# A 2-layer hybrid diffusion step on one core: the attention stage's products with the values moved between the two scores of a group

## The chip, the cores and the metric

The kernel runs on one core of one Trainium2 chip. The metric is device microseconds (us) of one launch; lower is better. The engines are named as in the trace: PE is TensorE (PEld its weight loads), DVE is VectorE, ACT is ScalarE, POOL is GpSimd, and SP is SyncE, which here only starts DMAs. Each engine works through its own list of instructions in the order in which the program wrote it, and waits between engines are semaphores that count up.

## The reference, cut to what matters

The step has two layers: a long gated convolution with its feed-forward block, and then a neighbourhood attention with its feed-forward block. Only the attention of the second layer is touched. 16 heads of 64 values each attend over 1024 latent tokens on a 16 x 64 grid; a block of queries sees a window of local keys and all 256 cached context keys in one softmax. The 256 prompt tokens of the same layer attend among themselves.

```python
s_loc = einsum('bhrjqd,bhrjkd->bhrjqk', qb, kg) + bias
s_loc = where(valid, s_loc, -inf)
s_ctx = einsum('bhrjqd,bhkd->bhrjqk', qb, k_ctx)
p = softmax(concatenate([s_loc, s_ctx], axis=-1))
o = p[..., :nk] @ vg + p[..., nk:] @ v_ctx
```

## The kernel before

All matrices go through TensorE as a high and a low part (`_hi`, `_lo`), so that a product of two of them is three matmuls. The attention is one stage of the program (lines 1973 to 2343). It takes the heads in 8 pairs `i`. A pair has U = 20 units `u` of 128 queries, 10 for each head of the pair, and G = 10 groups `g` of two units. In each head, groups 0 to 3 are local (640 scores a query: 256 of the context and 384 of the window), and group 4 is the prompt (256 scores a query). Five groups, thus one head, are called a half here; there are 16 halves in the stage.

A unit passes through these steps, each a function of its own:

- `scores` (PE, L2126): six matmuls, or two for the prompt, into `ps_s[u % 2]`.
- `minima` (DVE, L2292): bias and mask are added and the row minimum of the negated scores taken; the result lies in `probs`.
- `exps` (ACT, L2198): the exponential with its row sum, in place.
- `recip` (DVE, L2299) and `norm` (POOL, L2261): division by the sum. POOL also makes the bias of later units (`bias_mask`, L2252).
- `turn_local` (three transposes a unit into `ps_l`) and `turn_ctx` (four a group into `ps_c`), both PE, L2130.
- `high_local`, `high_ctx` (ACT, L2204, L2211) and `low_local`, `low_ctx` (DVE, L2303, L2308): the transposed numbers split into `pt_hi` and `pt_lo`.
- `mix` (PE, L2171), once a group: the products with the values, 18 matmuls for a local group and 6 for the prompt, into `ps_o`, of which there is one.
- `out_high` (ACT, L2217) and `out_low` (DVE, L2315): `ps_o` is read out into `a_hi` and `a_lo`. `mix(i, g)` waits on the semaphore `ol_ok` until `out_low` of group g - 1 is through, since it writes `ps_o` anew. It also waits on `ll_ok` and `lc_ok` for its own `pt_lo`.

`run` (L2052) calls one function `step(i, g, last)` on each engine, in the same sequence; what stands in an engine's `step` is the order of its queue. Step g of PE makes the scores of group g + 1, turns group g and mixes group g - 1. ACT's step g is `high_local(2g)`, `exps(2g + 2)`, `high_local(2g + 1)`, `high_ctx(g)`, `exps(2g + 3)`, `out_high(g - 1)`. DVE's step g is the following, where `out_low` is two groups back:

```python
if scored(g, last):
    minima(i, 2 * g + 2)
if g >= 2:
    out_low(i, g - 2)
if turned and local(2 * g):
    low_local(i, 2 * g)
if scored(g, last):
    minima(i, 2 * g + 3)
    recip(i, 2 * g + 2)
```

After these come `low_local(2g + 1)`, `low_ctx(g)` and `recip(2g + 3)`; at the last group of a pair `out_low(9)` stands at the end of the step.

Of the kernel before, what the change touches and what calls it, by code (L numbers as in the profile page):

```python
# [53 lines left out]
def hyena_natten_step(nc, t):  # L54
    ctx = ExitStack()
    with ctx:
# [1916 lines left out]
        with stage() as st:  # L1973
# [30 lines left out]
            def unit(u):  # L2004

                hh, n = u % U // 10, u % 10
                return (hh, n // 2, n % 2) if n < 8 else (hh, None, n - 8)

            def local(u):
                return unit(u)[1] is not None  # L2010

            def locals_before(u):

                return sum(local(v) for v in range(u))

            def unit_at(i, c):
                return i * U + c

            def local_at(i, c):
                return i * 16 + c  # L2020

            def group_at(i, c):
                return i * G + c
# [28 lines left out]
            def run(eng, prologue, step):  # L2052

                prologue()
                step(0, 0, False)
                for i in range(7):
                    for g in range(1, G + 1):
                        step(i, g, False)
                for g in range(1, G + 1):
                    step(7, g, True)  # L2060

            def scored(g, last):

                return not (last and g >= G - 1)
# [42 lines left out]
            def _(pe):  # L2107
# [21 lines left out]
                def turn(dst, u, b):  # L2129
                    return pe.transpose(dst, pb[:, u % U % 4, 128 * b:128 * b + 128], ident[:, :])  # L2130

                def turn_local(i, u):
                    pe.wait_ge(pn_ok, unit_at(i, u + 1))
                    if u >= 2:
                        pe.wait_ge(ll_ok, local_at(i, locals_before(u - 1)))
                    for b in range(3):
                        last = turn(ps_l[u % 2][:, 128 * b:128 * b + 128], u, 2 + b)
                    last.then_inc(tl_mm, 1)

                def turn_ctx(i, g):  # L2140
                    if g:
                        pe.wait_ge(lc_ok, group_at(i, g))
                    for half in range(2):
                        pe.wait_ge(pn_ok, unit_at(i, 2 * g + half + 1))
                        for b in range(2):
                            last = turn(ps_c[:, 256 * b + 128 * half:256 * b + 128 * half + 128], 2 * g + half, b)
                        last.then_inc(tc_mm, 1)

                def mix(i, g):
                    hh, j, _ = unit(2 * g)  # L2150
                    if g == 0:
                        pe.wait_ge(v_in[4 + i % 2], 16 * (i // 2) + 16)
                    if hh == 0:
                        if j is None:
                            pe.wait_ge(v_in[6 + i % 2], 16 * (i // 2) + 16)
                        else:
                            pe.wait_ge(v_in[j], i * 64 + 64)
                    if j is not None:
                        pe.wait_ge(ll_ok, local_at(i, locals_before(2 * g + 2)))
                    pe.wait_ge(lc_ok, group_at(i, g + 1))  # L2160
                    pe.wait_ge(ol_ok, group_at(i, OL0 + g))
                    s, c = 6 * (g % 2), 14 + 4 * (g % 2)
                    v0 = (16 if j is not None else 18) + 4 * (i % 2)
                    uses = [(v0, c, 0, 256)]
                    if j is not None:
                        uses += [(4 * j, s, 0, 128), (4 * j + 3, s + 7, 128, 128), (4 * j + 1, s + 2, 0, 256),
                                 (4 * j + 2, s + 4, 0, 256)]
                    uses += [(v0 + 1, c + 2, 0, 256)]
                    for n, (b, x0, q0, nq) in enumerate(uses):
                        for term, (hl, x) in enumerate(((0, pth), (0, ptl), (1, pth))):  # L2170
                            last = pe.matmul(ps_o[:, q0:q0 + nq], vt[:, b, hl, :],  # L2171
                                             x[:, x0:x0 + nq // 128, :].rearrange("p a b -> p (a b)"),
                                             start=n == 0 and term == 0, stop=n == len(uses) - 1 and term == 2)
                    last.then_inc(pv_mm, 1)
# [6 lines left out]
                def step(i, g, last):  # L2181
                    for half in range(2):
                        if scored(g, last):
                            scores(i, 2 * g + 2 + half)
                        if local(2 * g) and not (last and g == G):
                            turn_local(i, 2 * g + half)
                    if not (last and g == G):
                        turn_ctx(i, g)
                    if g:
                        mix(i, g - 1)  # L2190
                run(pe, prologue, step)

            @block.scalar
# [85 lines left out]
            @block.vector  # L2279
            def _(dve):  # L2280
                def minima(i, u):
                    w = width(u)
                    dve.wait_ge(s_mm, unit_at(i, u + 1))
                    if local(u):
                        dve.wait_ge(bm_ok, local_at(i, locals_before(u) + 1))
                    else:
                        dve.wait_ge(bm_ok, local_at(i, locals_before(u)))
                    before = u - 4
                    if before >= 0:
                        dve.wait_ge(tc_mm, unit_at(i, before + 1))  # L2290
                    dve.sem_inc(turn_v, 1)
                    dve.tensor_tensor_reduce(out=pb[:, u % U % 4, 0:w], in0=ps_s[u % 2][:, 0:w], in1=bm[:, u % 2, 0:w],  # L2292
                                             scale=1.0, scalar=3.0e38, op0=ALU.add, op1=ALU.min,
                                             accum_out=stat[:, u % 4, 0:1]).then_inc(sm_ok, 1)

                def recip(i, u):
                    q = stat[:, u % 4, :]
                    dve.wait_ge(p_exp, unit_at(i, u + 1))
                    dve.reciprocal(q[:, 2:3], q[:, 1:2]).then_inc(rr_ok, 1)  # L2299

                def low_local(i, u):
                    dve.wait_ge(hl_ok, local_at(i, locals_before(u) + 1))
                    dve.tensor_tensor(p_loc(ptl, u), ps_l[u % 2][:, 0:384].rearrange("p (b n) -> p b n", n=128),  # L2303
                                      p_loc(pth, u).bitcast(F32), ALU.subtract).then_inc(ll_ok, 1)

                def low_ctx(i, g):
                    dve.wait_ge(hc_ok, group_at(i, g + 1))
                    dve.tensor_tensor(p_ctx(ptl, g), ps_c[:, :].rearrange("p (b n) -> p b n", n=128),  # L2308
                                      p_ctx(pth, g).bitcast(F32), ALU.subtract).then_inc(lc_ok, 1)

                def out_low(i, g):
                    dve.wait_ge(oh_ok, group_at(i, g + 1))
                    dst, src = views(a_l, i, g)
                    hi = views(a_h, i, g)[0]
                    dve.tensor_tensor(dst, src, hi.bitcast(F32), ALU.subtract).then_inc(ol_ok, 1)  # L2315

                def prologue():
                    dve.sem_inc(ol_ok, OL0)
                    minima(0, 0)
                    minima(0, 1)  # L2320
                    recip(0, 0)
                    recip(0, 1)

                def step(i, g, last):
                    turned = not (last and g == G)
                    if scored(g, last):
                        minima(i, 2 * g + 2)
                    if g >= 2:
                        out_low(i, g - 2)
                    if turned and local(2 * g):  # L2330
                        low_local(i, 2 * g)
                    if scored(g, last):
# [3 lines that stand above are left out]
                        low_local(i, 2 * g + 1)  # L2336
                    if turned:
                        low_ctx(i, g)
                    if scored(g, last):
                        recip(i, 2 * g + 3)  # L2340
                    if g == G:
                        out_low(i, G - 1)
                run(dve, prologue, step)

        stage_rest(1, e0)
# [143 lines left out]
```

## Time and profile before

| | us |
|---|---|
| median of 3 runs | 3808.89 (3808.26 to 3813.37) |
| the profiled execution, device time | 3808.96 |
| its span in the trace | 3807.1 |
| attention stage in it, first scores to last product | 2322.1 to 2695 |
| PE busy over the whole span | 3598.1 (95%) |

A stage of the program ends with a barrier, so what the attention stage gains or loses is added to the whole one for one. In a row of the timeline the first number is the start and the second the duration, both in us; a matmul's end is a modelled one, and matmuls overlap, so that the distance between two starts tells more than one duration. What stands in brackets is how long the engine had been idle, and which instruction released it.

### The profile page before, as it was taken

How to read it: one execution, taken by the hardware profiler on the slowest of the kernel's cores; microseconds unless marked ns; L12 is line 12 of the kernel's file. 1: busy time of each engine (PE TensorE's matmuls, PEld its weight loads, DVE VectorE, ACT ScalarE, POOL GpSimd, SP SyncE). 2: the span in 40 equal slices, each digit the busy share in tenths (PEclk: the TensorE clock that was granted, in tenths of full speed). 3: DMA queues.
4: the chain of work that ended last, by engine and by line, in shares of the span. 5: the costliest groups of instructions: out<-in, count | busy, mean ns of one | idle time of the engine just before them, and what ended most of it. 6: DMA issues, size and time to landing. Idle time of an engine off the chain costs nothing. (4 is left out here: it accounts for less than half of the span.)

```text
span 3807.1 us, 47310 instructions
## 1 busy us (share of the span) xinstructions
PE 3598.1 (95%) x19244; PEld 3065.7 (81%) x19244; DVE 1515.6 (40%) x2472; ACT 1033.6 (27%) x1554; POOL 1230.0 (32%) x815
## 2 busy tenths in 40 slices
PE   8999998898899999999989998999899999999997
PEld 6788887677788888888868877888778888888885
DVE  2765553454524444434451014777341122111116
ACT  1441111132421111111152224777433111111113
POOL 1531113623532222222361213666343222222223
PEclk9999999999999999999999999999999999999998
DMA  3253323754122122221234355777201111111111
GB/s 118 87 168 117 105 90 134 247 187 145 49 72 67 61 78 72 76 68 62 77 120 161 144 174 158 179 178 171 84 28 39 35 39 39 39 38 35 39 39 61
DMA packets 178710, 369.58 MB, mean 97 GB/s; under 512 B 17063, under 2 KB 102567, under 8 KB 176840
## 3 DMA queue, kind: packets, MB, share of 16 engines
q1 hardware_dynamic: 173064, 356.21, 29.7%
q10 hardware_dynamic: 5440, 10.49, 0.9%
q8 instruction: 146, 2.39, 0.3%
q14 instruction: 60, 0.49, 0.0%
HBM read 286.93 MB, written 79.69 MB: 96 GB/s over the span
## 5 line engine op out<-in xcount | busy, mean ns | idle before, releaser
L148 POOL TENSOR_TENSOR w_lo<-w_raw,w_hi 128x1024 fp32r<-128x1024 f32 x210 | 506.0, 2410 | 1509.1 <-ACT w_hi L142 1509.1
L156 PE MATMUL ps_r<-a_hi,w_hi 128*128 128x512 f32 (+1 forms) x2496 | 640.4, 358 | 17.1 <-POOL a_lo L1716 11.4
L156 PE MATMUL ps_r<-a_hi,w_lo 128*128 128x512 f32 (+1 forms) x2496 | 635.8, 356 | 0.0
L156 PE MATMUL ps_r<-a_lo,w_hi 128*128 128x512 f32 (+1 forms) x2496 | 635.6, 356 | 0.0
L142 ACT ACTIVATE w_hi<-w_raw 128x1024 fp32r<-128x1024 f32 (+1 forms) x217 | 225.3, 1038 | 1018.3 <-PE ps_r L156 563.4
L156 PEld LDWEIGHTS ps_r<-a_hi,w_hi 128*128 128x128 f32 x2496 | 415.2, 188 | 100.3 <-POOL a_lo L1716 19.2
L156 PEld LDWEIGHTS ps_r<-a_lo,w_hi 128*128 128x128 f32 x2496 | 415.1, 188 | 74.0 <-issue 1.5
L156 PEld LDWEIGHTS ps_r<-a_hi,w_lo 128*128 128x128 f32 x2496 | 415.1, 188 | 73.6
L1909 DVE TENSOR_TENSOR hid_l<-hid_l,ps_r 128x1280 f32<-128x1280 f32 x44 | 65.5, 1488 | 840.7 <-PE ps_r L156 840.7
L1929 DVE SCALAR_TENSOR_TENSOR x_t_l<-ps_r,mod,x_t_l 128x1024 f32<-128x1024 f32 (+1 forms) x288 | 241.4, 880 | 264.6 <-PE ps_r L156 264.6
L1756 POOL TENSOR_TENSOR hid_lo_l<-hid_l,hid_hi_l 128x1280 fp32r<-128x1280 f32 x42 | 134.4, 3201 | 488.1 <-ACT hid_hi_l L1657 488.1
L156 PE MATMUL ps_in<-x_split_f,w_hi 128*128 128x512 f32 (+1 forms) x1152 | 259.7, 361 | 2.6 <-DVE gout_f L571 2.6
L1846 DVE CUSTOM_DVE_ANT_0 ps_x<-ada_w_l,silu_c_l 128x1024 f32<-128x1024 f32 x116 | 198.4, 1710 | 110.0 <-DMA ada_w_l<-in_ada_t 107.5
L156 PEld LDWEIGHTS ps_in<-x_split_f,w_hi 128*128 128x128 f32 x1152 | 192.2, 191 | 36.5 <-DVE gout_f L571 2.8
L156 PE MATMUL ps_r<-hid_hi_l,w_lo 128*128 128x512 f32 (+1 forms) x864 | 214.2, 355 | 0.0
L156 PE MATMUL ps_r<-hid_hi_l,w_hi 128*128 128x512 f32 (+1 forms) x864 | 214.2, 355 | 0.0
L156 PE MATMUL ps_r<-hid_lo_l,w_hi 128*128 128x512 f32 (+1 forms) x864 | 214.2, 355 | 0.0
L1657 ACT ACTIVATE hid_hi_l<-hid_l 128x1280 fp32r<-128x1280 f32 x44 | 56.1, 1274 | 541.8 <-DVE hid_l L1909 541.8
L1651 ACT ACTIVATE hid_l<-ps_r 128x1280 f32<-128x1280 f32 x44 | 54.6, 1240 | 455.2 <-PE ps_r L156 455.2
L2171 PE MATMUL ps_o<-pt_hi,v_hl 128*128 128x256 f32 (+1 forms) x832 | 166.6, 289 | 7.6 <-DVE a_lo L2315 7.6
L1461 PE MATMUL ps_r<-a_hi,w_hi 128*128 128x512 f32 (+1 forms) x384 | 144.2, 376 | 23.6 <-PEq L78 14.1
L156 PEld LDWEIGHTS ps_r<-hid_lo_l,w_hi 128*128 128x128 f32 x864 | 142.1, 188 | 25.5
(227 smaller groups left out, 6038.2 us busy)
## 6 DMA issues: line engine op xcount, KB each, us to landing
w_raw<-in_w_all SPq DMA_DIRECT2D x213, 512.0 KB, 3.6
ada_w_l<-in_ada_t SPq DMA_DIRECT2D x59, 512.0 KB, 3.5
v_hl<-v_d SPq DMA_DIRECT2D x128, 128.0 KB, 2.9
t_tail_f<-in_ada_t SPq DMA_DIRECT2D x24, 512.0 KB, 4.2
spec<-gout_f SPq DMA_DIRECT2D x80, 128.0 KB, 2.1
g_spec_c<-spec ACTq DMA_DIRECT2D x20, 512.0 KB, 5.7
y_d<-y_spec_c SPq DMA_DIRECT2D x40, 256.0 KB, 3.5
v_d<-z_v_l SPq DMA_DIRECT2D x10, 1024.0 KB, 4.6
```

What stands on the lines that cost most here:

```text
L142: act.activation(wh[:, s, 0:width], raw[:, s, 0:width], ACT.Copy).then_inc(w_hi, 1)
L148: pool.tensor_tensor(wl[:, s, 0:width], raw[:, s, 0:width], wh[:, s, 0:width].bitcast(F32), ALU.subtract).then_inc(w_split, 1)
L156: last = pe.matmul(out[:, c0:c1], w[:, c % 2, blk * 128:blk * 128 + 128], x[:, c0:c1], start=start and b == 0 and term == 0, stop=stop and ...
L1461: last = pe.matmul(bank(n, c1 - c0), w[:, (e0 + m) % 2, k * 128:k * 128 + 128], x[:, k, c0:c1], start=k == 0 and term == 0, stop=k == KT - ...
L1651: act.activation(sg[:, :], pg[0][:, 0:TOK], ACT.Silu).then_inc(silu, 1)
L1657: act.activation(hh[:, i % 2, k, :], sg[:, :], ACT.Copy).then_inc(hh_ok, 1)
L1756: pool.tensor_tensor(hl[:, i % 2, k, :], sg[:, :], hh[:, i % 2, k, :].bitcast(F32), ALU.subtract).then_inc(hl_ok, 1)
L1846: dve.tensor_tensor_reduce(out=px[:, :], in0=w[:, :], in1=vec[:, q, :], scale=1.0, scalar=0.0, op0=ALU.mult, op1=ALU.add, accum_out=acc_a[ ...
L1909: dve.tensor_tensor(sg[:, :], sg[:, :], pg[1][:, 0:TOK], ALU.mult).then_inc(gated, 1)
L1929: ins = dve.scalar_tensor_tensor(xt[:, m, p0:p1], pg[m % 2][:, p0:p1], gate[:, p:p + 1], xt[:, m, p0:p1], ALU.mult, ALU.add)
L2171: last = pe.matmul(ps_o[:, q0:q0 + nq], vt[:, b, hl, :], x[:, x0:x0 + nq // 128, :].rearrange("p a b -> p (a b)"), start=n == 0 and term = ...
```

## The change

On PE the products with the values of group g - 1 move from the end of step g to a place behind the transposes of the group's first unit, between the two scores. On DVE `out_low(g - 2)` moves ahead of the first `minima` of the step. ACT, POOL and SP keep their lists as they are.

```diff
@@ -2184,10 +2184,10 @@
                             scores(i, 2 * g + 2 + half)
                         if local(2 * g) and not (last and g == G):
                             turn_local(i, 2 * g + half)
+                        if g and half == 0:
+                            mix(i, g - 1)
                     if not (last and g == G):
                         turn_ctx(i, g)
-                    if g:
-                        mix(i, g - 1)
                 run(pe, prologue, step)
@@ -2323,10 +2323,10 @@
                 def step(i, g, last):
                     turned = not (last and g == G)
+                    if g >= 2:
+                        out_low(i, g - 2)
                     if scored(g, last):
                         minima(i, 2 * g + 2)
-                    if g >= 2:
-                        out_low(i, g - 2)
                     if turned and local(2 * g):
                         low_local(i, 2 * g)
```

PE's list, at a step that makes the prompt's scores (two matmuls each). Before, from the first transposes to the start of the mix:

```order
L2126 MATMUL ps_s<-k_hl_193_16730,q_hl_192_16729 128x256 x2
L2130 MATMUL ps_l<-ident,probs_16724 128x128 x3
L2126 MATMUL ps_s<-k_hl_193_16730,q_hl_192_16729 128x256 x2
L2130 MATMUL ps_l<-ident,probs_16724 128x128 x3
L2130 MATMUL ps_c<-ident,probs_16724 128x128 x4
L2171 MATMUL ps_o<-pt_hi_16725,v_hl_16723 128x256
```

The same step in the changed program, with the first and the last matmul of the mix:

```order
L2126 MATMUL ps_s<-k_hl_193_16730,q_hl_192_16729 128x256 x2
L2130 MATMUL ps_l<-ident,probs_16724 128x128 x3
L2171 MATMUL ps_o<-pt_hi_16725,v_hl_16723 128x256
...
L2171 MATMUL ps_o<-pt_hi_16725,v_hl_16723 128x256
L2126 MATMUL ps_s<-k_hl_193_16730,q_hl_192_16729 128x256 x2
L2130 MATMUL ps_l<-ident,probs_16724 128x128 x3
L2130 MATMUL ps_c<-ident,probs_16724 128x128 x4
```

The mix now stands ahead of one score, three transposes and the four context transposes that it stood behind.

DVE's list at the seam of two local steps, before (L2292 is `minima` and the reading of its result, L2315 `out_low`, L2303 `low_local`, L2308 `low_ctx`):

```order
L2308 TENSOR_TENSOR pt_lo_16726<-ps_c,pt_hi_16725 128x512
L2299 RECIPROCAL stat_16728<-stat_16728 128x1
L2292 ISA probs_16724,stat_16728<-ps_s,bias_m_16727 128x640
L2292 ISA stat_16728 128x1
L2315 TENSOR_TENSOR a_lo<-ps_o,a_hi 64x16x16
L2303 TENSOR_TENSOR pt_lo_16726<-ps_l,pt_hi_16725 128x3x128
```

and in the changed program:

```order
L2308 TENSOR_TENSOR pt_lo_16726<-ps_c,pt_hi_16725 128x512
L2299 RECIPROCAL stat_16728<-stat_16728 128x1
L2315 TENSOR_TENSOR a_lo<-ps_o,a_hi 64x16x16
L2292 ISA probs_16724,stat_16728<-ps_s,bias_m_16727 128x640
L2292 ISA stat_16728 128x1
L2303 TENSOR_TENSOR pt_lo_16726<-ps_l,pt_hi_16725 128x3x128
```

`out_low` changed places with one `minima`; what lies before and behind the two is the same. ACT's list, which is the same in both programs, ends a local step like this (L2204 is `high_local`, L2211 `high_ctx`, L2198 `exps`, L2217 `out_high`):

```order
L2204 ACTIVATE pt_hi_16725<-ps_l 128x3x128
L2211 ACTIVATE pt_hi_16725<-ps_c 128x512
L2198 ACTIVATE probs_16724,stat_16728<-probs_16724,stat_16728 128x640
L2217 ACTIVATE a_hi<-ps_o 64x16x16
```

## Rows read from the trace of the kernel before

**Rows 1.** Windows: two halves; busy PE, PEld, DVE, ACT, POOL, clock, DMA, GB/s.

```profile
2466.54:2511.42 44.88, 41.47 (x348) 39.99 (x348) 34.12 (x96) 31.88 (x76) 28.40 (x36) 1.00 0.73 175
```

**Rows 2.** Waits in the attention stage: us in total, times, longest us.

```profile
PE ps_l L2130 <- POOL probs L2261: 21.2, 47, 0.7
...
PE ps_o L2171 <- DVE a_lo L2315: 7.6, 16, 1.0
```

**Rows 3.** Timeline of all engines, last steps of a half and first of the next.

```profile
2505.34 0.40 PE L2126 MATMUL ps_s<-k_hl,q_hl 128*128 128x256 f32 x2
...
2511.42 0.43 DVE L2315 TENSOR_TENSOR a_lo<-ps_o,a_hi 64x256 fp32r<-64x256 f32 x1
...
2512.00 0.35 PE L2171 MATMUL ps_o<-pt_hi,v_hl 128*128 128x256 f32 x1 [0.50 <-DVE a_lo L2315]
...
2512.37 0.60 ACT L2211 ACTIVATE pt_hi<-ps_c 128x512 fp32r<-128x512 f32 x1
...
2513.00 0.69 DVE L2308 TENSOR_TENSOR pt_lo<-ps_c,pt_hi 128x512 fp32r<-128x512 f32 x1 [0.21 <-ACT pt_hi L2211]
```

**Rows 4.** Timeline of all engines, the local step that follows.

```profile
2514.17 0.82 PE L2126 MATMUL ps_s<-k_hl_l,q_hl_l 128*128 128x256 f32 x6
...
2515.09 0.90 PE L2126 MATMUL ps_s<-k_hl_l,q_hl_l 128*128 128x256 f32 x6
2515.20 0.82 DVE L2292 CUSTOM_DVE_ANT_0 probs<-ps_s,bias_m 128x640 f32<-128x640 f32 x1 [1.23 <-PE ps_s L2126]
...
2515.37 0.49 ACT L2204 ACTIVATE pt_hi<-ps_l 128x384 fp32r<-128x384 f32 x1 [0.62 <-PE ps_l L2130]
...
2516.07 0.83 ACT L2198 ACTIVATE probs<-probs,stat 128x640 f32<-128x640 f32 x1 [0.21 <-DVE stat L2292]
...
2516.17 0.60 PE L2130 MATMUL ps_c<-ident,probs 128*128 128x128 f32 x4
...
2516.64 0.35 PE L2171 MATMUL ps_o<-pt_hi,v_hl 128*128 128x256 f32 x1
...
2517.00 0.81 DVE L2292 CUSTOM_DVE_ANT_0 probs<-ps_s,bias_m 128x640 f32<-128x640 f32 x1
...
2517.43 0.82 PE L2126 MATMUL ps_s<-k_hl_l,q_hl_l 128*128 128x256 f32 x6
...
2518.11 0.80 POOL L2261 TENSOR_SCALAR probs<-probs,stat 128x640 f32<-128x640 f32 x1 [1.08 <-DVE stat L2299]
...
2518.80 0.38 ACT L2217 ACTIVATE a_hi<-ps_o 64x256 fp32r<-64x256 f32 x1
...
2518.96 0.55 PE L2130 MATMUL ps_l<-ident,probs 128*128 128x128 f32 x3 [0.71 <-POOL probs L2261]
...
2519.22 0.43 DVE L2315 TENSOR_TENSOR a_lo<-ps_o,a_hi 64x256 fp32r<-64x256 f32 x1 [0.19 <-ACT a_hi L2217]
```

**Rows 5.** Timeline of ACT alone, the end of a local step.

```profile
2494.31 0.47 ACT L2204 ACTIVATE pt_hi<-ps_l 128x384 fp32r<-128x384 f32 x1
2494.68 0.59 ACT L2211 ACTIVATE pt_hi<-ps_c 128x512 fp32r<-128x512 f32 x1
2495.16 0.82 ACT L2198 ACTIVATE probs<-probs,stat 128x640 f32<-128x640 f32 x1
...
2495.97 0.37 ACT L2217 ACTIVATE a_hi<-ps_o 64x256 fp32r<-64x256 f32 x1
```

**Rows 6.** Timeline, the stage's first half: its first `low_ctx`.

```profile
2331.41 0.69 DVE L2308 TENSOR_TENSOR pt_lo<-ps_c,pt_hi 128x512 fp32r<-128x512 f32 x1 [0.40 <-ACT pt_hi L2211]
```

**Rows 7.** Timeline, the first `minima` of the stage's second half.

```profile
2350.16 0.82 DVE L2292 CUSTOM_DVE_ANT_0 probs<-ps_s,bias_m 128x640 f32<-128x640 f32 x1 [5.64 <-POOL bias_m L2252]
```

**Rows 8.** Timeline of PE, the last mix of the stage.

```profile
2694.47 0.35 PE L2171 MATMUL ps_o<-pt_hi,v_hl 128*128 128x256 f32 x1 [1.02 <-DVE a_lo L2315]
```

**Rows 9.** Windows, columns as in Rows 1: a window with idle time, one at low clock.

```profile
1010.00:1015.00 5.00, 3.07 (x15) 2.19 (x13) 5.00 (x9) 3.43 (x5) 5.00 (x4) 1.00 0.00 0
...
2350.00:2355.00 5.00, 3.85 (x17) 3.48 (x18) 2.93 (x8) 2.33 (x5) 4.90 (x7) 0.50 1.00 239
```

## The prediction, made before the changed kernel was run

> **What bounds the kernel now.** I first asked for the busy time of a steady piece of the attention stage, since the change touches no other. Two halves (two heads) last 44.88 us, and PE is busy for 41.47 us of it, 92%, at the full granted clock, 1.00; DVE is busy 34.12 us, ACT 31.88 us and POOL 28.40 us [rows 1]. A half therefore takes 22.44 us and PE bounds it. Then I read the waits of the stage: what PE loses is 21.2 us in 47 transposes that came before POOL had normalised the unit, and 7.6 us in 16 mixes that waited for `out_low` [rows 2]. Together that is 28.8 us, and no reordering of PE can win more than about that here. Last I read the timeline of single steps, because the change shifts a mix by a fraction of a step and the answer lies in distances of tenths of a us.
>
> **What the change removes.** In a step of before, the two scores stand close together (starts 2514.17 and 2515.09 [rows 4]) and then comes the mix. With the mix between the scores, POOL gets some 2.2 us more for the second unit, so most of the 21.2 us can go. `out_low` ahead of `minima` could also take the 7.6 us. That is the gain, at most 28.8 us.
>
> **What it adds: the mix meets a wait that it did not meet before.** `mix(g)` needs `out_low(g-1)`. That one needs `out_high(g-1)`, and ACT's list was left as it is: `out_high(g-1)` stands at the end of ACT's step g, behind `high_local(2g+1)`, `high_ctx(g)` and `exps(2g+3)`. `exps(2g+3)` needs `minima(2g+3)`, which needs the second score of step g. So in the changed program each mix waits for a chain that begins at the end of the second score before it, and the next second score stands behind that mix on PE. This is a loop through four engines. Before, a whole mix and a second score lay in the same distance on PE and hid it.
>
> I work the chain out from e, the end of the second score. Distances between starts:
>
> - The first unit's score of 2514.17 ends at 2514.99; `minima` starts at 2515.20, that is e + 0.21, and `exps` 0.87 after it, at e + 1.08 [rows 4]. So far DVE's side.
> - ACT's side: transposes right behind a score are seen by ACT at 2515.37, 0.38 after the score's end. The context transposes end at 2516.77, which is 0.78 after the end of the second score (2515.99) [rows 4]; ACT sees them 0.03 later, e + 0.81. `high_local` fits ahead of it (0.38 + 0.37 = 0.75, the 0.37 from [rows 5]). `high_ctx` to `exps` is 0.48, so `exps` starts at e + 1.29. This is later than 1.08 and decides.
> - `exps` to `out_high` is 0.81 [rows 5]: e + 2.10. `out_high` to `out_low` is 0.42 [rows 4]: e + 2.52. `out_low` to the first matmul of the mix is 0.58 [rows 3]: e + 3.10. DVE is free for `out_low` in time: `low_ctx` starts at about e + 1.57 and takes 0.69, and the reciprocal behind it is over by e + 2.5.
>
> **The cover.** Between e and its mix, PE has the transposes to e + 0.78 and then the first score of the next step with its three transposes, 0.92 (from 2514.17 to 2515.09 [rows 4]): 1.70 us. The hold of 3.10 leaves 1.4 us idle in each local step. Part of it will be spent before the transposes: the next unit's reciprocal now stands behind the `minima` of e + 0.21, `norm` starts 1.11 after such a `minima` (2517.00 and 2518.11) and the transposes 0.85 after `norm` (2518.96) [rows 4], so at e + 2.17, and they end at 2.72, still 0.38 ahead of the mix. The wait for POOL thus gets longer than before and costs nothing, as long as the hold is above 2.7.
>
> **The sum for a half.** From the start of a mix of 18 matmuls to the next score it is 2.17 us (2512.00 to 2514.17 [rows 3, 4]), with the score of 0.82 it is 2.99 to the next e. If the prompt's score follows (0.40 [rows 3]) it is 2.57. The prompt's own mix is 0.79 (2516.64 to 2517.43 [rows 4]), with a local score 1.61.
>
> - Mixes of groups 0 and 1: 3.10 + 2.99 = 6.09 each.
> - Mix of group 2: 3.10 + 2.57 = 5.67.
> - Mix of group 3: `exps` is the prompt's and some 0.33 shorter, which would give 2.77; but `low_ctx` (0.63 behind `high_ctx`, 0.69 long [rows 3]) and the reciprocal hold DVE until about e + 2.27, and 0.58 more is 2.85. 2.85 + 2.99 = 5.84.
> - Mix of group 4: there is no `high_local`, and DVE's side decides: 1.08 + 0.81 + 0.42 + 0.58 = 2.89. 2.89 + 1.61 = 4.50.
>
> Sum 28.19 us, against 22.44 us before: 5.75 us more a half, PE busy at 41.47 / 2 = 20.7 of 28.2 us, 74%.
>
> **The ends.** In the first half the first `low_ctx` starts at 2331.41 [rows 6]; the first mix needs only that (no `out_low` precedes it): 2331.41 + 0.69 + 0.15 = 2332.25. The way to the mix of group 3 is 2.99 + 3.10 + 2.99 + 3.10 + 2.57 + 2.85 = 17.60, so it starts at 2349.9. The `minima` beside it is that of the second half's first unit, which in before stood idle 5.64 us for its bias table until 2350.16 [rows 7]. So the first half's extra time is hidden in a wait for a DMA that exists anyway. From 2349.9, 14 halves of 28.19 give 2744.6; then 2.99 + 4.50 + 6.09 + 6.09 + 5.67 lead to the last score at 2769.9, 2.85 + 2.17 to the end of the mix of the last local group, and about 2.5 (transposes 0.62, `high_ctx`, `low_ctx`, `out_low`, 0.58) to the last mix at 2777.4. Before, it started at 2694.47 [rows 8]. The difference is 83 us. The profiled execution of before took 3808.96 us, the median is 3808.89, so no correction: 3808.96 + 83 = **3892 us**. The feed-forward stage behind moves as a block.
>
> **Bounds of what no row shows.** That `high_ctx` starts 0.03 after the transposes end, and the DVE terms of groups 3 and 4, are put together from neighbouring steps. If each of some 75 holds is 0.2 us shorter, the sum falls by 15 us, and with a little less in the seams to 3868; 0.3 longer gives 3915, and some steps at the low clock 3925.
>
> **Rivals.**
>
> *The clock falls (chance 0.06).* PE then idles twice in a step, for about 1 us and 0.4 us. At the low clock 17 matmuls took 3.85 us, 0.226 each [rows 9], and at the full one 348 took 41.47, 0.119 each [rows 1]. The 24 matmuls from mix to e would cost 24 x 0.107 = 2.6 us more. If a third of 75 steps ran so, 25 x 2.6 = 65 us, 3957 us; if all, about 4070. Against it: PE was busy only 3.07 of 5 us in one window, 61%, and the granted clock stayed 1.00; it was 0.50 in a window of the stage's start, where PE had stood for DMAs [rows 9]. The trace of before has no long stretch of regular short gaps, so it isn't excluded. The Trainium skill, "TensorE: Matmul & The Clock Gate", section "A second HAM failure mode: psum-queue depth-cycling", says that a kernel whose PE idled briefly and often between groups of matmuls had its clock swing between the two levels; the window at 61% does not agree with that.
>
> *Only `low_ctx` holds the mix (0.05).* If `out_high` were off the loop, for instance since ACT reaches it sooner than I think, the mix could start when its own `pt_lo` is there: 1.57 + 0.69 + 0.15 = e + 2.41, 0.7 less a step, 75 x 0.7 = 52 less: 3840 us. ACT's list speaks against it.
>
> *The wait is covered and the gain stays (0.03).* This is the other side. If the chain ended within PE's cover, mixes would start at once, and PE's 28.8 us of waits would go: 3780 us. It decides at a hold of 1.70 us; `exps` alone starts at 1.29 and its way to the mix is 1.81, so it would need `out_low` to be free of `exps`.
>
> *Nothing moves (0.02).* The lists of PE and DVE show that the mixes and `out_low` did move, so only a gain and a loss of like size could give it: about 3809 us.
>
> **How the numbers follow.** The forecast (3868 to 3925 around 3892) has 0.84. The range 3868 to 3925 leaves out 0.16: the clock above, 3840, 3809 and 3780 below. About 0.2% (8 us) is what a measurement of this kernel can tell from no change. Slower: 0.84 + 0.06 + 0.05 = 0.95. Same 0.02, faster 0.03.
>
> **What the new profile would show.** Two halves should last about 56.4 us with PE at 74% and clock 1.00. The wait "PE `ps_o` for DVE `a_lo`" should grow from 16 to some 75 entries of about 0.4 us or a little more, 30 to 40 us, and the wait of `ps_l` for POOL to some 60 entries of about 1 us; in the timeline `out_high` should start right behind `exps`, 0.81 after it, and `out_low` 0.42 later, and the waits of ACT's `a_hi` for `ps_o` should be gone. I am wrong if the mixes start without a wait, if `out_high` starts earlier than the `exps` ahead of it in the list, or if the clock of the stage falls under 0.95.

## The result, and the profile of the changed kernel

The changed kernel takes 3927.81 us (median of 4 runs, 3921.97 to 3931.66), against 3808.73 us before: a ratio of 1.0309, with a 95% interval of 1.0291 to 1.0326. It is 119 us slower. The forecast was slower by 83 us, 3892 us, with a range up to 3925; the time lies 3 us above the range.

The profiled execution took 3931.66 us, its span is 3929.8 us. First what answers to [rows 1], a window over one pair of heads (two halves), with the columns as there.

```profile
2517.80:2579.20 61.40, 48.17 (x348) 45.03 (x348) 35.19 (x97) 32.89 (x77) 28.52 (x37) 0.92 0.53 129
```

The same 348 matmuls that took 44.88 us in [rows 1] now take 61.40 us. The forecast was 56.4 us at a granted clock of 1.00; the clock is 0.92. The waits of the stage (us in total, times, longest us), which answer to [rows 2]:

```profile
PE ps_l L2130 <- POOL probs L2261: 57.0, 64, 1.2
PE ps_o L2171 <- DVE a_lo L2315: 49.7, 70, 2.1
```

Nearly each mix now waits for `out_low` (70 times and not 16), and the transposes wait for POOL longer than before (57.0 us and not 21.2). Then the loop itself, in the timeline of one step at the full clock. It is the step that leads from the prompt's mix at the end of a pair to the first mix of the next pair; it answers to [rows 3 to 5]:

```profile
2569.20 0.28 PE L2171 MATMUL ps_o<-pt_hi,v_hl 128*128 128x256 f32 x1
...
2569.32 0.82 PE L2126 MATMUL ps_s<-k_hl_l,q_hl_l 128*128 128x256 f32 x6
...
2570.52 0.49 ACT L2204 ACTIVATE pt_hi<-ps_l 128x384 fp32r<-128x384 f32 x1 [0.32 <-PE ps_l L2130]
...
2570.96 0.60 ACT L2211 ACTIVATE pt_hi<-ps_c 128x512 fp32r<-128x512 f32 x1
...
2571.45 0.82 ACT L2198 ACTIVATE probs<-probs,stat 128x640 f32<-128x640 f32 x1
...
2572.32 0.55 PE L2130 MATMUL ps_l<-ident,probs 128*128 128x128 f32 x3 [0.75 <-POOL probs L2261]
2572.39 0.38 ACT L2217 ACTIVATE a_hi<-ps_o 64x256 fp32r<-64x256 f32 x1
...
2572.80 0.43 DVE L2315 TENSOR_TENSOR a_lo<-ps_o,a_hi 64x256 fp32r<-64x256 f32 x1 [0.24 <-ACT a_hi L2217]
...
2573.37 0.36 PE L2171 MATMUL ps_o<-pt_hi,v_hl 128*128 128x256 f32 x1 [0.50 <-DVE a_lo L2315]
```

The second score ends at e = 2570.14. `high_ctx` starts at e + 0.82 (forecast 0.81), `exps` at e + 1.31 (1.29), `out_high` at e + 2.25 (2.10), `out_low` at e + 2.66 (2.52), the mix at e + 3.23 (3.10). `out_high` had nothing to wait for but its turn in ACT's list: the last matmul into `ps_o` started at 2569.20 and was over at 2569.48, 2.9 us before `out_high` read it.

This hold is one of the longer kind. At the full clock a local step of the first head has `exps` at e + 1.32, `out_high` at e + 2.13 and the mix at e + 3.09, within 0.03 us of the forecast at each point. In the second head, and at the seam shown, `out_high` comes 0.93 us after `exps` and not 0.81, and the mix starts at e + 3.24.

And the starts of five mixes in a row, in the same trace:

```profile
2547.76 0.36 PE L2171 MATMUL ps_o<-pt_hi,v_hl 128*128 128x256 f32 x1 [0.51 <-DVE a_lo L2315]
...
2555.52 0.35 PE L2171 MATMUL ps_o<-pt_hi,v_hl 128*128 128x256 f32 x1 [0.95 <-DVE a_lo L2315]
...
2562.53 0.35 PE L2171 MATMUL ps_o<-pt_hi,v_hl 128*128 128x256 f32 x1 [1.48 <-DVE a_lo L2315]
...
2568.53 0.36 PE L2171 MATMUL ps_o<-pt_hi,v_hl 128*128 128x256 f32 x1 [0.28 <-DVE a_lo L2315]
```

The distances are 7.76, 7.01 and 6.00 us, and 4.84 to the mix at 2573.37. The forecast for the first three was 6.09 (mix of group 1 to that of group 2), 5.42 (2.57 + 2.85) and 5.88. So two of the steps are 1.6 to 1.7 us longer than forecast, and the third is 0.1 us longer. The windows over them say why (columns as in [rows 1]; the last but two is the clock):

```profile
2550.00:2553.00 3.00, 3.00 (x18) 3.00 (x17) 0.91 (x3) 0.47 (x1) 0.00 (x0) 0.56 0.31 87
2553.00:2556.00 3.00, 1.33 (x10) 0.92 (x9) 2.44 (x7) 2.42 (x7) 1.67 (x3) 1.00 0.27 88
2556.00:2559.00 3.00, 3.00 (x16) 3.00 (x16) 0.31 (x1) 0.47 (x2) 0.82 (x1) 0.51 0.00 0
```

PE ran at the low level, 1.2 GHz, for most of the first and the third window. Each of them follows a mix that had been held (idle 0.51 us before 2547.76, and 0.95 us before 2555.52). In the second window PE was back at 2.4 GHz. A low stretch sits on the mix and on the second score, which are both in the loop. From the second pair on the lengths of the ten steps repeat within 0.15 us, with the low clock at the same three of them (6.88, 7.75 and 7.01 us). The last mix of the stage starts at

```profile
2814.71 0.36 PE L2171 MATMUL ps_o<-pt_hi,v_hl 128*128 128x256 f32 x1 [1.96 <-DVE a_lo L2315]
```

and not at 2694.47 [rows 8]: 120 us of the 123 us that the span has grown.

### The profile page after: what moved, and what is told of

Same layout as the page of the kernel before. It is cut to its first block and busy times, and to the rows that moved or that the text cites. A ratio compares the mean times of both kernels' runs of the same rounds, so it can differ in the third digit from the quotient of the medians.

```text
span 3929.8 us, 47310 instructions
## 1 busy us (share of the span) xinstructions
PE 3649.8 (93%) x19244; PEld 3105.4 (79%) x19244; DVE 1521.6 (39%) x2472; ACT 1040.0 (26%) x1554; POOL 1229.6 (31%) x815
## 5 line engine op out<-in xcount | busy, mean ns | idle before, releaser
L156 PE MATMUL ps_r<-a_hi,w_hi 128*128 128x512 f32 (+1 forms) x2496 | 642.8, 359 | 16.6 <-POOL a_lo L1716 10.5
L2171 PE MATMUL ps_o<-pt_hi,v_hl 128*128 128x256 f32 (+1 forms) x832 | 186.7, 312 | 50.9 <-DVE a_lo L2315 49.7
L2171 PEld LDWEIGHTS ps_o<-pt_hi,v_hl 128*128 128x128 f32 x832 | 150.5, 214 | 66.1 <-issue 63.9
L2261 POOL TENSOR_SCALAR probs<-probs,stat 128x640 f32<-128x640 f32 (+1 forms) x160 | 117.6, 735 | 240.8 <-DVE stat L2299 240.0
L2292 DVE CUSTOM_DVE_ANT_0 probs<-ps_s,bias_m 128x640 f32<-128x640 f32 (+1 forms) x160 | 118.4, 740 | 180.7 <-PE ps_s L2126 167.7
```

The lines of the kernel that those rows point to most:

```text
L156: last = pe.matmul(out[:, c0:c1], w[:, c % 2, blk * 128:blk * 128 + 128], x[:, c0:c1], start=start and b == 0 and term == 0, stop=stop and ...
L2171: last = pe.matmul(ps_o[:, q0:q0 + nq], vt[:, b, hl, :], x[:, x0:x0 + nq // 128, :].rearrange("p a b -> p (a b)"), start=n == 0 and term = ...
L2261: pool.tensor_scalar(p, p, stat[:, u % 4, 2:3], 1.0, ALU.mult, ALU.mult).then_inc(pn_ok, 1)
```

## The experiments

The main theory has two parts. First, the loop through `exps`, `out_high` and `out_low` holds every mix. Second, PE's idle time in this loop lets the clock fall. The rivals were that the mix waits for `low_ctx` only, and that the clock has no part in it.

**Each half of the change alone.** `e1_dve_only` has PE's list of before and this on DVE:

```diff
                     turned = not (last and g == G)
+                    if g >= 2:
+                        out_low(i, g - 2)
                     if scored(g, last):
                         minima(i, 2 * g + 2)
-                    if g >= 2:
-                        out_low(i, g - 2)
```

> Only DVE's half of the change: out_low(g-2) ahead of the step's first minima, PE's order as before. Theory (each mix is held by the chain exps, out_high, out_low, but before a whole mix of PE covered it): out_low comes up to 0.86 us earlier, the 16 waits of the mix for it (7.6 us) go, and minima starts at most a few tenths later under cover: about 3802 us. Rival (DVE's move is what delays the minima and so the whole loop): slower than 3809 by tens of us.

Measured: 3793.15 us against 3807.97 us of before on the same chip, ratio 0.9964 (0.9953 to 0.9976). The same edit once more, beside the two variants at the end of this section:

> DVE's half of the change alone, once more, beside the two variants below: 3793 us as in its first run, 0.3 to 0.4% under before.

Measured: 3796.11 us against 3810.97 us, ratio 0.9957 (0.9945 to 0.9969). So DVE's half alone is faster than before by 15 us, twice what I expected. Its waits in the trace of the first run:

```profile
PE ps_l L2130 <- POOL probs L2261: 14.2, 41, 0.9
...
PE ps_o L2171 <- DVE a_lo L2315: 1.4, 2, 1.0
...
DVE a_lo L2315 <- ACT a_hi L2217: 42.6, 72, 2.6
```

The 7.6 us of waits for `a_lo` went to 1.4, as expected; those for POOL also fell, from 21.2 to 14.2 us, which I had not foreseen, and no run separates why. DVE itself now stands 42.6 us for ACT, at a place where this costs little: while the mix runs, no new score is there for `minima`.

`e2_pe_only` is the other half, the mix between the scores with `out_low` where it was.

```diff
+                        if g and half == 0:
+                            mix(i, g - 1)
                     if not (last and g == G):
                         turn_ctx(i, g)
-                    if g:
-                        mix(i, g - 1)
```

> Only PE's half: the mix between the two scores, out_low still behind the first minima. Loop theory: out_low then starts behind a minima of 0.83 us, so that each hold grows from 3.10 to about 3.88 us after the second score; 75 holds give about 58 us more than the changed kernel: about 3986 us, more if the clock falls further. Rival (the mix waits for low_ctx only): like the changed kernel, about 3928 us.

Measured: 4004.46 us against 3807.97 us, ratio 1.053 (1.0505 to 1.0555). The seam of a step shows the added term: the `minima` now stands inside the chain, between `exps` and `out_low`.

```profile
2485.01 0.82 ACT L2198 ACTIVATE probs<-probs,stat 128x640 f32<-128x640 f32 x1
...
2485.83 0.36 ACT L2217 ACTIVATE a_hi<-ps_o 64x256 fp32r<-64x256 f32 x1
...
2486.22 0.43 DVE L2292 CUSTOM_DVE_ANT_0 probs<-ps_s,bias_m 128x256 f32<-128x256 f32 x1
...
2486.57 0.41 DVE L2315 TENSOR_TENSOR a_lo<-ps_o,a_hi 64x256 fp32r<-64x256 f32 x1
...
2487.13 0.36 PE L2171 MATMUL ps_o<-pt_hi,v_hl 128*128 128x256 f32 x1 [0.69 <-DVE a_lo L2315]
```

`out_high` starts at 2485.83 and `out_low` could start 0.41 later, at 2486.24; it starts at 2486.57 behind a prompt unit's `minima` of 0.43, and a local unit's takes 0.82. The added term was to give 58 us over the changed kernel, and it is 77. Two things make this up, and no run prices them apart. Where the clock is full, the first two mixes of a pair are 6.83 us apart against 6.09 in the changed kernel, 0.74 us more (0.78 expected), but a local step of the second head takes 6.56 against 6.23, only 0.33 us more. And the clock is lower: 0.87 from 2400 to 2640 us of the trace, where the changed kernel has 0.91. The rival that only `low_ctx` holds the mix falls: it gave 3928 us.

**Taking `exps` out of the loop.** `e3_act_early` changes ACT's list only:

```diff
                     if scored(g, last):
                         exps(i, 2 * g + 2)
+                    if g:
+                        out_high(i, g - 1)
                     if turned and local(2 * g):
                         high_local(i, 2 * g + 1)
...
                     if scored(g, last):
                         exps(i, 2 * g + 3)
-                    if g:
-                        out_high(i, g - 1)
```

> The changed kernel, with out_high(g-1) moved ahead of high_local(2g+1) on ACT, so that it is done before the second score's exps. If ACT's list alone sets the hold, the mix starts when low_ctx is done, e + 2.41 instead of e + 3.10: about 3875 us. My theory says that DVE's list holds it as well, since out_low stands behind recip(2g+3), which needs the same exps and ends at e + 2.46: hold about 3.04, a gain of only 5 us, about 3922 us.

Measured: 3888.47 us, ratio 1.0211 (1.0192 to 1.0231). This lies between the two and needs two readings. Where its clock is full, a local step takes 5.88 us in the first head and 6.03 in the second, against 6.09 and 6.24 in the changed kernel: 0.2 us less, not 0.7. DVE's list does hold the mix, as the theory had it: `out_low` starts right behind `recip(2g+3)`, which needs the same `exps`.

```profile
2564.33 0.82 ACT L2198 ACTIVATE probs<-probs,stat 128x640 f32<-128x640 f32 x1
...
2565.27 0.16 DVE L2299 RECIPROCAL stat<-stat 128x1 f32<-128x1 f32 x1
2565.35 0.40 DVE L2315 TENSOR_TENSOR a_lo<-ps_o,a_hi 64x256 fp32r<-64x256 f32 x1
...
2565.89 0.36 PE L2171 MATMUL ps_o<-pt_hi,v_hl 128*128 128x256 f32 x1
```

The other part of the gain is the clock, which is 0.94 to 1.00 in windows of 30 us from 2400 to 2640 (0.98 over all of them) and not 0.91; a low stretch shows in 4 of its steps behind the first half, and in 22 of the changed kernel's.

`e4_act_dve_early` moves `out_low` too, into the same step:

```diff
                     if turned and local(2 * g):
                         low_local(i, 2 * g)
+                    if g:
+                        out_low(i, g - 1)
                     if scored(g, last):
                         minima(i, 2 * g + 3)
```

with the other two calls of `out_low` taken out, and ACT's list as in the run before.

> The changed kernel with out_high(g-1) ahead of high_local(2g+1) on ACT and out_low(g-1) in the same step on DVE, between low_local(2g) and minima(2g+3). Loop theory: no exps lies in the loop any more, the hold is low_ctx's, e + 2.41 (e + 1.95 for the prompt's group), a half takes 24.7 us at the full clock: about 3842 us, up to 3860 with some steps at the low clock. The waits of ps_o for a_lo become waits for pt_lo. Rival (out_low is not what holds the mix): about 3928 us.

Measured: 3859.04 us, ratio 1.0145 (1.0128 to 1.0162). The waits for `a_lo` are gone and the step is 5.48 to 5.52 us, where 2.41 + 2.99 = 5.40 was expected. The term that sets it is another one than I named:

```profile
2566.94 0.80 POOL L2261 TENSOR_SCALAR probs<-probs,stat 128x640 f32<-128x640 f32 x1 [2.21 <-DVE stat L2299]
...
2567.79 0.55 PE L2130 MATMUL ps_l<-ident,probs 128*128 128x128 f32 x3 [0.77 <-DVE pt_lo L2308]
...
2568.10 0.36 PE L2171 MATMUL ps_o<-pt_hi,v_hl 128*128 128x256 f32 x1
```

The transposes come when POOL is done (2566.94 + 0.80, the next start 0.85 behind; the wait is put down to `pt_lo`, which ended at the same time), and the mix stands behind them. The second score before them ends at 2565.58, so the transposes start at e + 2.21 and the mix at e + 2.52, where the forecast had 2.17 for the transposes and 2.41 for the mix. So even without the wait for `out_low` the place between the scores is poor: the mix stands in PE's list behind transposes that wait for the reciprocal, and the next second score stands behind the mix.

**The clock.** `e5_after_fill` and `e6_after_fill_small` are the changed kernel with more work: transposes of a constant tile into columns of `ps_s1` that nobody reads.

```diff
+                def filler(i, g, n):
+                    pe.wait_ge(sm_ok, unit_at(i, 2 * g + 2))
+                    for _ in range(n):
+                        pe.transpose(ps_s[1][:, 640:768], ident[:, :], ident[:, :])
...
+                        if g and half == 0 and not (last and g >= G - 1):
+                            filler(i, g, 8)
                         if local(2 * g) and not (last and g == G):
                             turn_local(i, 2 * g + half)
+                        if g and half == 0 and not (last and g >= G - 1):
+                            filler(i, g, 4)
```

> The changed kernel with 12 more transposes of a constant tile a step, into columns of ps_s1 that nobody reads: 8 behind the first score (0.7 us) and 4 ahead of the mix (0.35 us), inside PE's idle time. They only add work. If the idle time is what lets the clock fall, the granted clock of the stage goes back to 1.00, the steps of 6.9, 7.8 and 7.0 us become 5.4, 6.1 and 5.4, and a pair of heads takes about 56 us and not 61.4: about 3891 us, faster with more work. If the clock has no part in the time, or falls for another reason, 3928 us or more.

Measured: 3901.27 us, ratio to before 1.0248 (1.0231 to 1.0265).

> The same with only 3 and 1 added transposes a step (0.35 us of the 1.3 us idle). If the clock depends on how much PE works between the holds, some low stretches stay: between 3891 and 3928 us, my guess 3910. If any activity at all in the gap is enough, 3891 us.

Measured: 3900.64 us, ratio 1.0245 (1.0228 to 1.0262). More work is faster than the changed kernel by 27 us. A pair of the small version, three of its mixes, and the added transposes (L2135) of one step:

```profile
2517.00:2573.80 56.80, 48.90 (x391) 44.23 (x390) 35.02 (x96) 32.87 (x76) 28.62 (x36) 1.00 0.57 140
```

```profile
2503.87 0.35 PE L2176 MATMUL ps_o<-pt_hi,v_hl 128*128 128x256 f32 x1 [0.24 <-DVE a_lo L2324]
...
2507.97 0.55 PE L2135 MATMUL ps_s<-ident 128*128 128x128 f32 x3
...
2509.43 0.27 PE L2135 MATMUL ps_s<-ident 128*128 128x128 f32 x1
...
2509.95 0.35 PE L2176 MATMUL ps_o<-pt_hi,v_hl 128*128 128x256 f32 x1 [0.25 <-DVE a_lo L2324]
...
2515.28 0.36 PE L2176 MATMUL ps_o<-pt_hi,v_hl 128*128 128x256 f32 x1 [0.86 <-DVE a_lo L2324]
```

The clock is 1.00, a pair takes 56.8 us (61.4 in the changed kernel, 56.4 in the forecast), and the steps are 6.08 and 5.33 us. The wait is still there; only its price is that of the loop alone. Both sizes do the same, so the four added transposes are as good as twelve. This settles that the clock fell because of PE's idle time in the loop, and prices it: 3927.81 - 3900.64 = 27 us by the medians. In the profiled executions it is more: from the first mix of the stage to the last it is 484.2 us in the changed kernel, 450.9 with twelve transposes and 448.6 with four, thus 33 to 36 us. The profiled execution of the changed kernel was the longest of its four (3931.66), and that of the small version the shortest (3893.22); what else makes the two prices differ was not settled.

**Other places for the mix.** `e7_mix_second` puts it behind the second score, with DVE's half of the change:

```diff
                             scores(i, 2 * g + 2 + half)
+                        if g and half == 1:
+                            mix(i, g - 1)
                         if local(2 * g) and not (last and g == G):
                             turn_local(i, 2 * g + half)
```

> Mix behind the second score and ahead of the second unit's transposes, out_low first in DVE's step, ACT's list as before. The wait for low_ctx is covered (2.35 us of PE work), but exps(2g+3) now stands behind high_ctx, which waits for the mix: the loop is mix 2.17, transposes 0.78, high_ctx 0.48, exps 0.81, out_high 0.42, out_low 0.58 = 5.2 us a step against 4.6: about 3850 us. Rival (only the cover of low_ctx matters): about 3795 us, like the kernel with DVE's half alone.

Measured: 3855.37 us, ratio 1.0126 (1.0109 to 1.0143). This is near the 3850 us of the loop and far from the rival's 3795; the local steps are 5.40 us in the first head and 5.55 in the second, 0.2 to 0.35 us more than the 5.2 expected.

`e8_mix_second_all` has new lists on ACT and DVE as well (the order is in its expectation).

> As the run before, with ACT's list as exps(2g+2), exps(2g+3), out_high(g-1), high_local(2g+1), high_ctx(g) and DVE's as minima, low_local, minima, both recips, out_low(g-1), low_local, low_ctx. Nothing in the loop of the mix then waits behind an exps that waits for the mix, and the reciprocals come early enough for POOL. PE should be the bound again, about 21.1 us a half: 3785 us, faster than both kernels. Rival (DVE, busy 83%, becomes late with low_ctx ahead of the next minima): 3800 to 3830 us.

Measured: 3829.99 us, ratio 1.0057 (1.004 to 1.0073). The rival was right. In its waits up to 2690 us DVE stands 64.4 us for `exps` to take the reciprocals, `low_ctx` is late for it, and PE waits for that:

```profile
DVE stat L2298 <- ACT probs L2198: 64.4, 90, 0.9
...
PE ps_o L2171 <- DVE pt_lo L2307: 23.8, 29, 1.1
```

**Two tries to go below the 3793 us.** Both start from DVE's half alone. `e10_exps_early` puts `exps(2g+3)` ahead of `high_ctx(g)` and `recip(2g+3)` ahead of `low_ctx(g)`; `e11_exps_first` puts both ahead of `high_local(2g+1)` and `low_local(2g+1)` too.

> DVE's half alone, and exps(2g+3) ahead of high_ctx(g) on ACT with recip(2g+3) ahead of low_ctx(g) on DVE. POOL gets the second unit some 0.5 us earlier, so that most of PE's 14.2 us of waits for POOL should go, and low_ctx has a whole step of slack: about 3785 us. Rival (out_high and low_ctx, now later, hold the mix again): 3795 us or more.

Measured: 3797.57 us against 3810.97 us, ratio 0.9963 (0.9951 to 0.9975), no different from DVE's half alone. PE's waits for POOL did not fall (14.7 us in 37 waits): some steps became shorter and others longer.

> The same with exps(2g+3) and recip(2g+3) still earlier, ahead of high_local(2g+1) and low_local(2g+1): DVE then stands idle for the exps before low_local, about 0.9 us a step of its 18% idle time. 3783 us if DVE has the room, 3800 us or more if it has not.

Measured: 3818.75 us, ratio 1.0019 (1.001 to 1.0027). DVE had not the room: up to 2690 us it waits 66.3 us for `exps`, and PE 24.5 us for POOL (14.7 us in the run before). DVE's half alone stays the best version, 0.4% faster than before and 3.4% faster than the changed kernel.

## Why the prediction missed its range

- **What bounds the kernel, and what the change removes.** Right in kind: PE's waits were 21.2 and 7.6 us, and DVE's half alone is 15 us faster. My reading that the gain on POOL's side comes from the mix between the scores was not borne out: with the mix there and nothing added, the waits for POOL grew in each run (57.0 us in the changed kernel), and they fell to 14.2 us with the mix where it was and `out_low` ahead of `minima`.
- **The loop.** Right. The hold was forecast at e + 3.10; it is 3.09 in the local steps of the first head, and 3.23 in the step shown and 3.24 in the second head. There the term that was too small is `exps` to `out_high`, 0.81 from [rows 5] and 0.94 here (2571.45 to 2572.39). At the full clock the steps are 6.09, 6.08, 5.32, 5.86 and 4.69 us in the first head (forecast 6.09, 6.09, 5.42, 5.88, 4.71), and up to 0.16 longer in the second. The sum of a pair is 56.8 us, not 56.4. The loop passes through PE, DVE and ACT, thus three engines and not four: POOL's wait lies beside it and ends before the mix.
- **The step that failed: the clock.** The sum took the full clock for every step, with only "some steps at the low clock" at the edge of the range. The low clock was a rival with a chance of 0.06, at 3957 us if a third of the steps were slow. Three steps in ten are slow, but each by about 1.5 us (7.75 against 6.22, 6.88 against 5.33), not by 2.6, since a low stretch ends within the step. By the medians 27 us of the 36 us by which the forecast was short are this. Against it I had set one window, at 61% busy with a clock of 1.00 [rows 9]. That was one idle stretch in another stage; the changed stage has two holds in every step, for 450 us. The Trainium skill, "TensorE: Matmul & The Clock Gate", section "A second HAM failure mode: psum-queue depth-cycling", which I named and set aside, describes a kernel whose PE idled briefly and often between groups of matmuls while its clock went back and forth between the two levels. This trace agrees: holds of at most 1.5 us in the steady steps, and a clock of 0.92. The fact that I had no row with regular short holds should have made the range wider, not the rival smaller.
- **The rest.** The medians leave about 9 us. The profiled executions close without them. There the last mix came 37.3 us later than forecast against the trace of before (120.2 and not 82.9 us). The mix of group 3 in the first half started at 2348.11, 1.8 us earlier than forecast. The loop's own terms, taken from the small filler run at the full clock, add 3.2 us in the 14 halves behind it and 0.4 us at the end. The other 35.5 us are what the changed kernel takes longer than the filler run over the same steps. It is more than the 27 us of the medians for the reason given with the filler runs, as far as that goes.
- **Slips that change little.** All 75 steps at the low clock would give 3892 + 75 x 2.6 = 4087 us, not 4070. The start of `low_ctx` at e + 1.57 follows from no row: 0.81 + 0.63 is 1.44, and it is 1.49 in the step shown (2571.63). The rival of `low_ctx` alone would have been some 10 us lower with 1.44.
- **The rivals.** That only `low_ctx` holds the mix was wrong: with PE's half alone the time is 4004 us, and with the mix between the scores it takes both of `e4`'s moves to reach even 3859. That the wait is covered was wrong, 70 mixes wait.
- **What the new profile would show.** The wait for `a_lo` was 49.7 us in 70 entries (forecast 30 to 40 in 75), the wait for POOL 57.0 in 64 (about 60 of 1 us), both right in place; the first is larger by a quarter than the upper end of what I gave. The condition "or if the clock of the stage falls under 0.95" was met: 0.92.

## What to carry to other kernels

When an instruction moves forward in one in-order list, follow each semaphore that it waits for back through the lists that were not changed: here the releasing step sat behind an unrelated `exps` on ACT, and that put a read-out whose input had been ready for 2.9 us into a loop through PE, DVE and ACT. Where an edit has parts in two queues, cost and run each by itself; the two-line move on DVE was the gain, and the move on PE hid it. And if a change gives TensorE short idle times in every step and no row shows what the clock does then, price the low clock into the range; here a few added transposes in the holds took it away.

## What the runs showed of the hardware

TensorE lost 27 us by the medians to its clock, in a stage where no single idle time in the steady steps was longer than 1.5 us and PE was busy for 78% of the time (48.17 of 61.40 us, the slow matmuls among them). Four more transposes of 128 columns a step (three in 0.55 us and one in 0.27 us in the rows above) kept the clock at 1.00 through the steps of the stage.

Two other kernels idle about as much. From 2400 to 2640 us the changed kernel has PE busy for 188.20 us at a clock of 0.91. ACT early alone (`e3`) has 190.37 us at 0.98, with a few low stretches, and DVE and ACT both early (`e4`) has 190.92 us at 1.00, with none. Why the changed kernel falls in the same three steps of every pair, and these do not, is left open.
